# Seven half-size products in place of eight in the conv feed-forward of a two-block kernel

## What is computed

```python
def conv_ffn(h, w_up, conv_w, conv_b, w_down, rows):
    u = h @ w_up
    ...
        u = conv2d_grid(u, conv_w, rows) + conv_b
    gate, val = jnp.split(u, 2, axis=-1)
    return (jax.nn.silu(gate) * val) @ w_down
...
        h = modulate(rms_norm(x, norm2_g[l]), sh2, sc2)
        x = x + g2 * conv_ffn(h, ffn_w_up[l], ffn_conv_w[l], ffn_conv_b[l], ffn_w_down[l], rows)
```

## Time and profile before

| | |
|---|---|
| median of 3 runs | 2053.72 us (2051.56 to 2055.73) |
| profiled execution | 2056.36 us, span of its instructions 2054.4 us |
| PE busy | 1844.3 us (90% of the span) |
| VectorE busy | 938.7 us (46%) |
| ScalarE busy | 401.8 us (20%) |
| GpSimd busy | 152.0 us (7%) |
| up stage, first matmul to the first of the down stage | 582.95 to 889.10 us |
| down stage, first matmul to its last | 889.10 to 1065.17 us |
| granted TensorE clock, mean | 0.943 of full speed |

### The profile page before, as it was taken

How to read it: one execution, slowest core, us unless ns; L and a number is a source line. 1 busy time by engine, 2 the same in 40 slices (tenths; PEclk the granted TensorE clock), 3 DMA queues, 4 the chain that set the end, 5 groups by cost and what they waited for, 6 DMA issues and landing times. The chain is left out here.

```text
span 2054.4 us, 27368 instructions
## 1 busy us (share of the span) xinstructions
PE 1844.3 (90%) x11650; PEld 1047.3 (51%) x11650; DVE 938.7 (46%) x1560; ACT 401.8 (20%) x740; POOL 152.0 (7%) x223
## 2 busy tenths in 40 slices
PE   6999759788999999999979999989988988878887
PEld 3554338676434444444538888865565333233332
DVE  2564196354349888950028559954443110101013
ACT  3222443234120111010113111253022000000001
POOL 0000002850000000000001100010000000000000
PEclk8999979798999999999989999999998999999999
DMA  8344004322311221135225522230538999999996
GB/s 318 139 184 153 21 21 108 82 53 78 106 60 67 82 82 68 63 102 193 87 82 200 210 103 82 98 109 21 208 149 319 427 426 426 426 426 425 427 427 251
DMA packets 80909, 375.40 MB, mean 183 GB/s; under 512 B 34336, under 2 KB 37408, under 8 KB 56848
## 3 DMA queue, kind: packets, MB, share of 16 engines
q1 hardware_dynamic: 68480, 344.56, 43.1%
q0 software_dynamic: 9552, 27.73, 3.8%
q10 hardware_dynamic: 2752, 1.31, 0.2%
HBM read 360.65 MB, written 18.87 MB: 185 GB/s over the span
## 5 line engine op out<-in xcount | busy, mean ns | idle before, releaser
L3113 PE MATMUL psum<-mem 128*64 128x512 f32 x1504 | 356.5, 630 | 36.3 <-DMA mem<-in_w_upe 16.3
L1962 PE MATMUL psum<-mem 128*128 128x512 f32 x704 | 305.0, 595 | 2.0 <-ACT mem L377 2.0
L1752 PE MATMUL psum<-mem 128*128 128x256 f32 x1120 | 250.4, 383 | 9.3 <-ACT mem L2330 4.9
L3113 PEld LDWEIGHTS psum<-mem 128*64 128x64 f32 x1504 | 117.9, 144 | 254.4 <-issue 250.9
L2028 DVE SCALAR_TENSOR_TENSOR mem<-mem 128x512 f32<-128x512 f32 x352 | 237.1, 750 | 0.0
L1752 PEld LDWEIGHTS psum<-mem 128*128 128x128 f32 x1120 | 212.7, 191 | 47.5 <-issue 13.9
L1962 PEld LDWEIGHTS psum<-mem 128*128 128x128 f32 x704 | 133.7, 190 | 172.7 <-issue 171.3
L574 PE MATMUL psum<-mem 128*128 128x512 f32 (+1 forms) x464 | 167.6, 523 | 2.1 <-ACT mem L377 2.0
L1408 PE MATMUL psum<-mem 128*128 128x512 f32 x352 | 156.0, 600 | 1.2 <-ACT mem L1984 1.2
L574 PEld LDWEIGHTS psum<-mem 128*128 128x128 f32 x464 | 87.9, 190 | 81.1 <-issue 72.1
L3175 DVE TENSOR_TENSOR mem<-mem,psum 128x512 f32<-128x512 f32 x16 | 11.0, 688 | 248.5 <-issue 217.9
(11 more groups left out here) (383 smaller groups left out, 2125.0 us busy)
## 6 DMA issues: line engine op xcount, KB each, us to landing
mem<-in_w_upe SPq DMA_DIRECT2D x31, 2048.0 KB, 27.5
mem<-in_w_gate SPq DMA_DIRECT2D x30, 2048.0 KB, 29.1
mem<-in_w_downe SPq DMA_DIRECT2D x29, 2048.0 KB, 32.2
mem<-in_ada SPq DMA_DIRECT2D x32, 1024.0 KB, 6.8
mem<-in_w_up SPq DMA_DIRECT2D x22, 1024.0 KB, 4.8
mem<-in_ada POOLq DMA_DIRECT2D x32, 512.0 KB, 4.8
mem<-in_w_in_g SPq DMA_DIRECT2D x12, 1024.0 KB, 4.9
mem<-in_w_down SPq DMA_DIRECT2D x16, 704.0 KB, 4.1
```

The costliest lines, as they stand in the source:

```text
L1752: last = pe.matmul(self.bank(q, n), left[:, kt], right[:, kt], start=n in (1, 2, 5) and kt == 0, stop=kt == self.tiles - 1, skip_group_che ...
L1962: last = pe.matmul(k.bank[2 * (m % 3) + h2][:, :], w[:, kt, h2], h[:, kt], start=kt == 0, stop=kt == KD - 1)
L3113: last = pe.matmul(bank[halves[h], :], xs[:, kt, halves[h]], pair[h][0][:, kt, cols], start=kt == 0, stop=kt == tiles - 1, skip_group_chec ...
```

## The change

Both products of the feed-forward go over to `Seven`: the up product with one pair (gate tile m and value tile m) as its two row blocks, 4 + 4 tiles of the 1024 channels and 256 + 256 tokens; the down product, in a new subclass `SevenDown`, with four pairs of output tiles, 11 + 11 tiles of `hidden` and 256 + 256 tokens. So each matmul has 256 columns, and there are 616 in the up product and 308 in the down product, where there were 352 and 176 of 512 columns.

Of the four quarters of a pair of grids, ACT copies the first part of each from its bank into the grid (`take`, after products 1, 5, 6 and 4), and DVE adds the second part onto it from its bank (`join`, after products 2, 3 and 7; product 4 needs none). The centre tap with the bias goes to ACT (`centre`), from the grid into a PSUM bank (4 to 7); DVE's eight other taps add to that bank, and the last value tap writes into `mem`. The SiLU reads the bank. The product of gate and value goes to GpSimd, and so do the weight sums of the up product, the first weight sums of the down product and its first column sum. `w_down` leaves the ring for five places of its own, and all `ada2` slots follow behind `w_up` in the ring; their rows are made ahead of and behind product 5(0) of the down stage. The residual is updated in place. The context's squares are made and summed in four steps instead of one.

```diff
@@ class Seven
-    def product(self, pe, q, n):
+    def product(self, pe, q, n, ready=None):
...
         for kt in range(self.tiles):
+            if ready:
+                ready(kt)
             last = pe.matmul(self.bank(q, n), left[:, kt], right[:, kt], start=n in (1, 2, 5) and kt == 0, stop=kt == self.tiles - 1,
                              skip_group_check=True)
...
+class SevenDown(SevenResidual):
...
+    def load(self, sp, q, i, j):
+        if (i, j) == (0, 0) and q:
+            sp.wait_ge(self.done[1], q)
+            sp.wait_ge(self.summed, 4 * q)
+        if (i, j) == (0, 1) and q:
+            sp.wait_ge(self.done[2], q)
+            sp.wait_ge(self.summed, 4 * q - 1)
+        if (i, j) == (1, 0) and q:
+            sp.wait_ge(self.summed, 4 * q)
+        if (i, j) == (1, 1) and q >= 2:
+            sp.wait_ge(self.done[4], q - 1)
+        sp.dma_start(self.slot(q, i, j), self.source(q, i, j)).then_inc(self.landed[i, j], 16)
...
+    def sum_3(self, eng, q):
+        eng.wait_ge(self.done[5], q + 1)
+        eng.tensor_tensor(self.s1, self.block(q, 0, 0), self.block(q, 1, 0), SUB).then_inc(self.summed, 1)
...
@@ class UpPads, ffn_stage
+    G, V = 2, 3
...
+        banks = ((4, 5), (6, 7))
+        self.sums = [lambda m, b=b: k.bank[b[m % 2]][:, :].rearrange("p (r c) -> p r c", r=ROWS) for b in banks]
...
-    pad = k.at(work, NP * 2 * PADW).rearrange("p (n h r c) -> p n h r c", n=NP, h=2, r=ROWS + 2)
-    acc = k.at(work + NP * 2 * PADW, 2 * 2 * SEQ).rearrange("p (n h r c) -> p n h r c", n=2, h=2, r=ROWS)
+    up = Seven(k, "w_up", 4, lambda q, i, j: w_up(q)[:, 4 * j:4 * j + 4, i], lambda i, j: h[:, 4 * i:4 * i + 4, 256 * j:256 * j + 256],
+               [three(25600 + 512 * i, 4, P) for i in range(3)], [three(21504 + 1024 * i, 4, 256) for i in range(4)], ((0, 1), (2,), (3,)))
...
+    down = SevenDown(k, "w_down", 11, places, lambda q, i, j: k.d["w_down"][2 * (2 * q + i) + j], half,
...
         @block.sync
         def _(sp):
-            k.send_weights(sp, k.number("w_down", 6))
-            sp.wait_ge(s["up_mm"], KF)
+            k.send_weights(sp, k.number("w_up", 8) + 1)
+            for i, j in ((0, 0), (1, 0), (1, 1), (0, 1)):
+                down.load(sp, 0, i, j)
+            down.load(sp, 1, 1, 1)
+            k.send_weights(sp, k.number("ada2", 7) + 1)
+            down.load(sp, 1, 0, 0)
+            down.load(sp, 1, 1, 0)
+            sp.wait_ge(s["hidden"], KF)
             sp.dma_start(context.x, k.d["ctx2"]).then_inc(context.landed, 16)
...
         @block.gpsimd
         def _(pool):
...
+            def product(m):
+                pool.wait_ge(s["silu"], m + 1)
+                pool.wait_ge(s["tap_v"], NT * (m + 1))
+                pool.tensor_tensor(hidden[:, m], pads.silu[m % 2], pads.value[m % 2], MUL).then_inc(s["hidden"], 1)
...
+            for q in range(KF):
+                if q >= 3:
+                    product(q - 3)
+                if q < LAST:
+                    landed(q + 1)
+                    up.sum_1(pool, q + 1)
+                    up.sum_2(pool, q + 1)
+                if q < LAST:
+                    up.sum_4(pool, q + 1)
+                    up.sum_3(pool, q + 1)
+                if q == LAST - 1:
+                    down.sum_1(pool, 0)
+            product(LAST - 2)
+            pool.wait_ge(up.done[4], KF)
+            pool.wait_ge(s["hidden"], 11)
+            down.turn_1(pool)
+            down.sum_2(pool, 0)
+            down.sum_4(pool, 0)
+            product(LAST - 1)
+            down.sum_3(pool, 0)
+            product(LAST)
 
         @block.tensor
         def _(pe):
-            for m in range(KF):
...
-                if m >= 3:
-                    pe.wait_ge(s["padded"], m - 2)
-                for h2 in range(2):
-                    for kt in range(KD):
...
-                        last = pe.matmul(k.bank[2 * (m % 3) + h2][:, :], w[:, kt, h2], h[:, kt], start=kt == 0, stop=kt == KD - 1)
-                last.then_inc(s["up_mm"], 1)
-            pe.wait_ge(s["padded"], KF)
-            down.products(pe)
+            for q in range(KF):
+                k.weights_ready(pe, k.number("w_up", q))
+                for n in (1, 2, 5, 6):
+                    up.product(pe, q, n, (lambda kt, first=4 * (n - 1): apply.ready(pe, first + kt, 0)) if q == 0 and n < 3 else None)
+                if q:
+                    up.product(pe, q - 1, 4)
+                up.product(pe, q, 3)
+                up.product(pe, q, 7)
+            up.product(pe, LAST, 4)
+
+            pe.wait_ge(up.taken[4], LAST)
+            pe.wait_ge(s["hidden"], 11)
+            down.product(pe, 0, 1)
...
+            mod.rows_by_product(pe, range(4))
+            pe.wait_ge(up.taken[4], KF)
+            down.product(pe, 0, 5)
+            mod.rows_by_product(pe, range(4, 8))
+            pe.wait_ge(s["hidden"], KF)
+            down.product(pe, 0, 2)
+            mod.turn(pe)
+            down.product(pe, 0, 6)
+            down.product(pe, 0, 3)
+            down.product(pe, 0, 7)
+            for q in range(1, ND):
...
         @block.scalar
         def _(act):
+            def take(q, n):
+                act.wait_ge(up.done[n], q + 1)
+                h2, j = {1: (0, 0), 6: (0, 1), 5: (1, 1), 4: (1, 0)}[n]
+                if n == 1 and q >= pads.G:
+                    act.wait_ge(s["tap_g"], NT * (q - pads.G + 1))
+                if n == 5 and q >= pads.V:
+                    act.wait_ge(s["tap_v"], NT * (q - pads.V + 1))
+                act.activation(pads.half(h2, q, j), rows4(up.bank(q, n)), ACT.Copy).then_inc(up.taken[n], 1)
...
+                act.activation(pads.sums[h2](m), pads.inner(h2, m), ACT.Identity, bias=k.v("ffn_conv_b", t),
+                               scale=k.v("ffn_conv_w", CENTRE * 2 * KF + t)).then_inc(s[("centre_g", "centre_v")[h2]], 1)
...
+            for q in range(KF):
+                if q:
+                    centre(0, q - 1)
+                take(q, 1)
+                if q >= 2:
+                    silu(q - 2)
+                take(q, 5)
+                take(q, 6)
+                if q:
+                    take(q - 1, 4)
+                    centre(1, q - 1)
...
         @block.vector
         def _(dve):
+            def tap(h2, m, i):
...
+                a = pads.sums[h2](m)
+                out = a
+                if h2 and i == NT - 1:
...
+                    out = pads.value[m % 2].rearrange("p (r c) -> p r c", r=ROWS)
...
+                dve.scalar_tensor_tensor(out=out, in0=pads.shifted(h2, m, TAPS[i]), scalar=w, in1=a, op0=MUL, op1=ADD).then_inc(done, 1)
...
+            def join(q, n):
+
+                h2, j, other = {2: (0, 0, 1), 3: (0, 1, 6), 7: (1, 1, 5)}[n]
+                at = pads.half(h2, q, j)
+                dve.wait_ge(up.taken[other], q + 1)
+                dve.wait_ge(up.done[n], q + 1)
+                dve.tensor_tensor(at, at, rows4(up.bank(q, n)), ADD).then_inc(up.taken[n], 1)
...
+                if kt == 6:
+                    dve.wait_ge(apply.done, 4)
+                    up.turn_1(dve)
+            dve.wait_ge(apply.done, KD)
+            up.turn_2(dve)
+            up.turn_3(dve)
+            up.turn_4(dve)
...
-            for m in range(KF):
-                dve.wait_ge(s["padded"], m + 1)
-                for i in range(9):
-                    for h2 in range(2):
...
-                    if i == 1 and m:
-                        product(m - 1)
-            product(KF - 1)
...
+            for m in range(KF + 1):
+                for i in range(NT):
+                    if m < KF:
+                        tap(0, m, i)
+                    if m:
+                        tap(1, m - 1, i)
+                    if i == 2 and m < LAST:
+                        join(m + 1, 2)
+                    if i == NT - 2 and m < LAST:
+                        join(m + 1, 3)
+                if m < LAST:
+                    join(m + 1, 7)
...
-    k.put("w_down", 0)
-    k.put("w_down", 1)
-    for m in range(1, KD):
-        k.put("w_down", 2 * m)
-        for g in MOD_PE[m]:
-            k.put("ada2", g)
-        k.put("w_down", 2 * m + 1)
+    for g in range(8):
+        k.put("ada2", g)
```

339 lines of the change are left out of this document (211 added, 128 removed).

## The result

The changed kernel takes **1997.45 us** (median of 4 runs, 1993.24 to 1999.61) beside 2054.56 us for the kernel before (2051.56 to 2055.73): 57.1 us less, a ratio of 0.9722, 95% interval 0.9702 to 0.9741. The forecast was 1996.5 in a range of 1989 to 2018. What follows asks how much of this agreement is the sum of the forecast, and how much is luck.

A forecast was written before the change was run, and what follows sets the result against it. PE was taken to bound the up and down stages. Savings of 35.7 (up), 21.2 (down) and 0.3 us (last addition) made 57.2, off the median 2053.7: 1996.5 us, with 1989 to 2018 for 8 in 10.

The forecast's parts named there:

- Up stage: Up product on PE: 306.15 us before, 270.4 after, so 35.7 us saved if PE stays the bound.
- price of a half product: A 256-column matmul on PE takes 0.2167 us, against 0.4325 for 512 columns; an up pair then takes 12.15 us.
- VectorE stays behind PE: Up stage: VectorE needs 11.9 us per pair against PE's 12.15 and follows with 0.2 us to spare.
- rival of an overhead for PSUM: Up stage: PSUM overhead makes a tap 0.734 us, a pair 12.75, 13 us lost, 2010; VectorE-bound chance 0.20.
- blocking rival: Up stage: GpSimd and VectorE block each other, 17.3 us per pair, 2110 us; slower beyond 14.8 per pair; chance 0.05.
- GpSimd's prices: GpSimd additions in up stage and passage: 1.08 us for 512 columns, 2.7 for 1408, 5.2 for 2816.
- T: End of 7(21), the up stage's last product on PE; the last `hidden` was forecast near T + 19.
- Down stage: Down product on PE: 176.07 us before, 154.9 after, so 21.2 us saved.
- 1 us for what a wait of this size does to the clock: Passage into the down stage: 1 us of lowered clock added to a 2.5 us stall for `ada2` weights.
- near 1008: Sign in the changed trace: the last down product stands near 1008 us.
- near 1414: Sign in the changed trace: the first expert weights are sent near 1414 us.
- second half of the claim: Behind the down stage: whatever the two stages save moves all that follows forward, one for one.

The follow-up runs named there:

- e_after_again: The changed kernel, unaltered, run again: 1991.34 us beside 2045.15 for the kernel before, ratio 0.9732.
- experiment 3: GpSimd's up-stage weight sums cut to 2 of 128 columns from the second pair: 12.12 us per pair with sums in PSUM, 12.6 in `mem`.
- e_passage: Changed kernel with three modulation rows ahead of 1(0), one behind, and the last value chain's first four taps one block earlier: 1991.04 us.
- first comparison: The first measurement of the changed kernel against the kernel before: 1997.45 us beside 2054.56, ratio 0.9722.
- e_down_eight: Changed kernel with the down product as eight blocks, 352 instructions of 512 columns, without weight sums or turns: 2007.06 us, 0.9810 to the kernel before.
- e_passage_sum: As e_passage, with GpSimd's fourth weight sum of the first down pair also behind the last `hidden`: 1989.86 us, 0.9726 to the kernel before.
- e_before_again: The kernel before, unaltered, profiled once more: 2050.90 us.
- e_sums_mem_thin: Changed kernel with convolution sums in `mem` and GpSimd's up weight sums cut to 2 of 128 columns from the second pair: 12.6 us per pair.

## Why the prediction was right, step by step

- **Up stage: right** (35.7 us forecast; 35.7 in the profile after, 36.2 in e_after_again). The price of a half product from another stage, 0.2167, held here: 12.12 us per pair for 12.15. The first pair came to 13.4 (267.93 - 21 x 12.12) for 13.5. In that pair GpSimd and VectorE did hold each other up: `turn_2` to `turn_4` took 2.09, 2.29 and 2.29 us where 1.22 was the price, more than the 0.6 us allowed for, yet they were ready in time for what needed them. The 0.58 us of waiting for join 7(21) were not in the sum; 21 pairs at 0.03 us less made up for them.
- **VectorE stays behind PE: right**, and as thin as said: 0.2 us of room forecast, 0.41 seen as idle time, and one operation of 0.6 us more per pair uses it up. The rival of an overhead for PSUM was priced from the Trainium skill ("Perfetto Trace Analysis", where the figures stand under "Optimizing Scalar/DVE Operations": about 125 ns for PSUM, 60 for SBUF, the on-chip memory that `mem` stands in). These runs show none of that difference: 0.66 us from tap to tap with the sum in PSUM, 0.669 over `mem`. The measurement decides.
- **The blocking rival: a real mechanism that the PSUM sums avoid.** It was put at 17.3 us per pair and a turning point of 14.8; with the sums in `mem` the pair is 16.7 and the kernel 46 us slower than before, where (16.7 - 14.8) x 22 = 42. The Trainium skill ("SBUF — State Buffer", "Who interferes with whom") has it that the second SBUF input is what contends; the runs agree in both directions (experiment 3). The change owes its gain to this as much as to the seven products.
- **GpSimd's prices: too low.** 1.28 us for 512 columns (1.08 forecast), 3.2 for 1408 (2.7), 6.19 for 2816 (5.2): the slope came from two rows at 768 and 1020 columns, and both are shorter than a line through the new rows would have them (1.83 and 2.37 us), for a reason not looked into. It cost nothing in the pairs and moved the last `hidden` to T + 20.9, where T + 19 was forecast. 2(0) starts later still (T + 23.6), but only because of the two waits for weights: in e_passage, where they are gone, the late `hidden` costs 1.17 us.
- **Down stage: the failed step is "1 us for what a wait of this size does to the clock".** 154.9 was forecast, this 1 us in it; 155.5 was measured where the clock stayed up, 160.0 where it fell and took 4.6 us, in two of three executions. It is no fixed price: 0 or 4.6, where the kernel before showed 0 or 1.7. The wait was right (3.0 for 2.5, for the reason given). That 14 runs of products each cost some 0.2 us at their start (22 instructions take 4.95 us to the next row, 44 take 9.72) was not in the sum, about 2.1 us; it was made up in part by the modulation rows, their turn and the sums, 16.8 us where 17.9 were taken, since they had been priced with their overlaps (153.9 + 2.1 + 0.5 - 1.1 = 155.4).
- **The sum: 57.2 forecast.** Measured in time 57.1 (first comparison) and 53.8 (second); by the stages the three profiles of after stand 53 us on average below the four of before (428.7 and 481.8). So the mechanism's size was overrated by some 4 us, all in the down stage, which saves 16.8 us on average for 21.2. Of these 4.4 us, some 2.0 are the clock of the changed kernel (3.0 lost on average for 1), 0.8 the clock of the kernel before, whose one profile at hand was one of the two with a loss, and 1.5 the longer wait and the starts of the products, less what the other rows gave. In the two profiles of the first comparison a start that was early by chance covered it; whether this holds for the medians, whose other executions left no trace, is not shown. The signs "near 1008" and "near 1414" came true (1006.21 and 1413.19) only with this early start. The second half of the claim holds: from the last down product to the first expert weights all seven profiles take 404.8 to 407.1 us, so what the stages save is passed on whole to that point. Behind the stages as a whole the three profiles of after take 2.6 us more on average than the four of before (991.6 and 989.0, the ranges touch); whether that is more than scatter stays open.

## What to carry to other kernels

When work moves to GpSimd beside a busy VectorE, look at where VectorE's operands stand before counting the work: with one input in PSUM the two ran side by side, with both in `mem` the same schedule took 4.6 us more per pair and turned a gain of 54 us into a loss of 46. Price an instruction from its densest row in another stage of the same trace; that held to 0.3% over 270 us, while small slopes drawn through two rows did not. And before a difference between two profiles is explained, profile one kernel several times: here the same code ahead of the change ended anywhere within 14 us.

## What the runs showed of the hardware

- The fall of TensorE's clock is no fixed price of a wait. Behind the same 2.9 us the kernel before kept its clock in two profiles and lost 1.7 us in two; behind 1.6 + 1.4 us and the turn the changed kernel lost some 4.6 us in two of three, with a granted clock of 0.70 from 863.0 to 874.3. It falls without any wait as well: in e_down_eight and e_passage_sum right behind the 32 narrow matmuls of the turn (L1435; 0.83 over 897 to 907 and 0.85 over 869 to 879), with PE never idle, and in all four profiles of before in the context's narrow sums (L1893; 0.50 over 1017.9 to 1020.6 in before, 0.56 over 1012.4 to 1015.0 in e_before_again). What decides it stays open.
- A GpSimd addition of eight columns took up to 3.8 us beside VectorE taps with both inputs in `mem`, for 0.22 us beside the others. The longest went from 707.40 to 711.22 in e_sums_mem_thin, across most of eight taps in a row, and ended as the join behind them began (711.07), which has only one input in `mem`. That looks like waiting, not like being slowed in proportion to its size.
